# GpSimd takes two of the eight residual additions behind each of three outputs

## The reference

```python
h = modulate(rms_norm_2(x, g_pre_ff1), sh1, sc1)
f = swiglu(h, w1_gate, w1_up, w1_down)
x = x + 0.5 * ga1[:, None, :] * rms_norm_2(f, g_post_ff1)      # first output
h = modulate(rms_norm_2(x, g_pre_mix), sh2, sc2)
...                                                            # attention and a state space branch
x = x + ga2[:, None, :] * rms_norm_2(mixed, g_post_mix)        # second output
h = modulate(rms_norm_2(x, g_pre_ff2), sh3, sc3)
f = swiglu(h, w2_gate, w2_up, w2_down)
x = x + 0.5 * ga3[:, None, :] * rms_norm_2(f, g_post_ff2)      # third output, the result
```

## Time and profile before

| what | us |
|---|---|
| median of 3 runs | 3137.19 (3136.27 to 3139.3) |
| profiled execution, its own time | 3139.77 |
| span of the profiled execution | 3137.7 |
| PE busy | 3002.3 (96%) |
| DVE busy | 1722.9 (55%) |
| ACT busy | 1008.0 (32%) |
| POOL busy | 217.0 (7%) |

### The profile page before, as it was taken

One profiled execution on the slowest core, in us unless ns is written; L12 is line 12 of the kernel. 1 busy time (PEld: TensorE's weight loads), 2 busy tenths in 40 slices (PEclk: granted clock), 3 DMA queues, 4 the chain that ended last, 5 costly groups with the idle time before them and its releaser, 6 DMA issues.

```text
span 3137.7 us, 51509 instructions
## 1 busy us (share of the span) xinstructions
PE 3002.3 (96%) x21594; PEld 2569.2 (82%) x21594; DVE 1722.9 (55%) x3294; ACT 1008.0 (32%) x1737; POOL 217.0 (7%) x446
## 2 busy tenths in 40 slices
PE   8999999999999998999999999999999898899997
PEld 7777998999999997788998888878888655578886
DVE  4564577547656336447755765657447453543334
ACT  4556232232212236542323222233222314432122
POOL 0130222000000100212210000000000000000000
PEclk9999999999999999999999999999999999999999
DMA  5201111235433320111123453422334311123232
GB/s 186 99 15 48 52 60 60 75 136 168 161 118 124 122 94 28 52 44 61 60 77 137 156 184 118 161 74 94 114 104 147 145 45 37 54 78 105 86 102 73
DMA packets 74494, 302.45 MB, mean 96 GB/s; under 512 B 10729, under 2 KB 11113, under 8 KB 69273
## 3 DMA queue, kind: packets, MB, share of 16 engines
q1 hardware_dynamic: 57880, 230.04, 22.1%
q0 software_dynamic: 16384, 69.13, 6.1%
HBM read 288.51 MB, written 14.63 MB: 97 GB/s over the span
## 4 chain that ended last, share of the span: by engine, by line
PE 88%; DVE 6%; ACT 4%; issue 1%; DMA 1%; POOL 0%; DVEq 0%; SPq 0%; ACTq 0%
PE acc L1066 18%; PE acc L1067 18%; PE acc L1068 18%; PE acc L1385 5%; PE acc L1386 5%; PE acc L1387 5%; PE acc L1085 2%; PE acc L1267 2%; ACT temps L1812 1%; PE acc L1241 1%; PE acc L1214 1%; PE acc L1613 1%; PE acc L1430 1%; PE acc L1451 1%; PE acc L1121 1%
## 5 line engine op out<-in xcount | busy, mean ns | idle before, releaser
L1067 PE MATMUL acc<-normed_r,toep_r 128*128 128x512 f32 (+1 forms) x1808 | 636.5, 352 | 0.0
L1735 ACT ACTIVATE toep_r<-ring 128x1024 fp32r<-128x1024 f32 (+2 forms) x340 | 392.9, 1157 | 695.3 <-PE acc L1068 676.1
L2230 DVE TENSOR_TENSOR ring_r<-ring,toep_r 128x1024 fp32r<-128x1024 f32 (+2 forms) x340 | 457.9, 1348 | 261.3 <-ACT toep_r L1735 261.0
L1067 PEld LDWEIGHTS acc<-normed_r,toep_r 128*128 128x128 f32 x1808 | 341.4, 189 | 45.1 <-issue 0.2
L1066 PE MATMUL acc<-mixed_r,toep_r 128*128 128x264 f32 (+1 forms) x1056 | 343.2, 325 | 0.7 <-DVE normed_r L2213 0.6
L1066 PE MATMUL acc<-work_r,toep_r 128*128 128x512 f32 (+1 forms) x988 | 342.1, 346 | 1.5 <-DVE ring_r L2230 1.4
L1068 PE MATMUL acc<-work_r,ring_r 128*128 128x512 f32 (+1 forms) x988 | 341.4, 346 | 0.0
L1068 PE MATMUL acc<-mixed_r,ring_r 128*128 128x264 f32 (+1 forms) x1056 | 339.3, 321 | 0.0
L1066 PE MATMUL acc<-temps_r,toep_r 128*128 128x512 f32 x752 | 298.3, 397 | 11.0 <-DVE normed_r L2216 8.3
L1067 PE MATMUL acc<-work_r,toep_r 128*128 128x512 f32 (+1 forms) x880 | 307.7, 350 | 0.0
L1385 PE MATMUL acc<-residual_r,toep_r 128*128 128x264 f32 (+1 forms) x1024 | 301.9, 295 | 3.7 <-ACT toep L1952 2.1
(11 more groups left out here) (432 smaller groups left out, 5296.8 us busy)
## 6 DMA issues: line engine op xcount, KB each, us to landing
ring<-in_w_pair SPq DMA_DIRECT2D x176, 512.0 KB, 3.5
ring<-in_w_down SPq DMA_DIRECT2D x64, 704.0 KB, 4.1
ring<-in_w_gb SPq DMA_DIRECT2D x64, 640.0 KB, 3.9
extra<-in_w_ada POOLq DMA_DIRECT2D x18, 1024.0 KB, 5.9
toep<-in_w_ada POOLq DMA_DIRECT2D x18, 1024.0 KB, 5.8
ring<-in_w_tm SPq DMA_DIRECT2D x24, 512.0 KB, 4.5
ring<-in_w_out SPq DMA_DIRECT2D x24, 512.0 KB, 3.5
ring<-in_w_fm SPq DMA_DIRECT2D x20, 512.0 KB, 3.9
```

What stands on the lines that cost most here:

```text
L1067: mm(out, wh, xl[:, a:z], start=False, stop=False)
L1735: A(high(ld), slot(ld), ACT.Copy).then_inc(S["w_high"], 1)
L2230: V.tensor_tensor(low(ld), slot(ld), high(ld), ALU.subtract).then_inc(S["w_low"], 1)
```

## The change

Tiles 2 and 5 of each of the three outputs are added by POOL. DVE still scales them, reports each on a new semaphore `term_made`, and goes on with the next tile without a wait; POOL waits for it, adds, and reports on `pool_added`. The list of what the next norm or the store waits for names `pool_added` for these two tiles. SP waits for both tiles of a pair. To have room for the two semaphores, four older ones become two (`start_args`, `start_exp`), `ang_ready` is folded into `ssm_args`, and an unused one goes.

```diff
+POOL_ADDS = (2, 5)
...
+            n["done"] = [mark("pool_added" if adds and i in POOL_ADDS else signal) for i in tiles] if signal else None
+            n["terms"] = [mark("term_made") for _ in POOL_ADDS] if adds else None
...
-        b2["post1"] = norm(Y, b2["ffn1"]["ready"], range(KT), TOKENS, "h_done", total=TMP)
+        b2["post1"] = norm(Y, b2["ffn1"]["ready"], range(KT), TOKENS, "h_done", total=TMP, adds=True)
...
+            def additions(n):
+
+                for event, k in zip(n["terms"], POOL_ADDS):
+                    wait(pool, event)
+                    nc.gpsimd.tensor_tensor(H[:, k, META:L], H[:, k, META:L], n["src"][:, k, META:L], ALU.add
+                                            ).then_inc(S["pool_added"], 1)
...
                 second_block()
+                for name in ("post1", "postmix", "post2"):
+                    additions(b2[name])
...
                 for i, k in enumerate(n["tiles"]):
-                    link(V.scalar_tensor_tensor(out=n["src"][:, k, a:z], in0=n["src"][:, k, a:z],
-                                                scalar=g[:, i:i + 1], in1=RINV[:, a:z], op0=ALU.mult, op1=ALU.mult))
+                    term = V.scalar_tensor_tensor(out=n["src"][:, k, a:z], in0=n["src"][:, k, a:z],
+                                                  scalar=g[:, i:i + 1], in1=RINV[:, a:z], op0=ALU.mult, op1=ALU.mult)
+                    if i in POOL_ADDS:
+                        term.then_inc(S["term_made"], 1)
+                        continue
+                    link(term)
...
-                    act.wait_ge(S["ang_ready"], 1)
+                    act.wait_ge(S["ssm_args"], 2)
...
-                act.wait_ge(S["lb_shift"], 1)
+                act.wait_ge(S["start_args"], 1)
...
-                act.wait_ge(S["lam_dots"], 1)
+                act.wait_ge(S["start_args"], 2)
...
-                wait(sp, b2["post2"]["done"][2 * i + 1])
+                for k in range(2 * i, 2 * i + 2):
+                    wait(sp, b2["post2"]["done"][k])
```

More of the change, by code:

```diff
@@ L453, in build @@
         names += """means_loaded params_loaded start_loaded consts_loaded params2_loaded row_ready masked_row_ready line_stored row_spread toep_loaded
-            constants_set start_used lb_shift lb_exp lam_dots lam_exp cact_ready""".split()
+            constants_set start_used start_args start_exp cact_ready""".split()
         names += """sq_ready sq_used mean_read stat_ready stat_rooted gate_scaled silu_ready""".split()
-        names += """weights_made joint_mean u_ready h_done f_done fm_ready tm_ready gate_ready act_ready
+        names += """weights_made joint_mean u_ready h_done f_done fm_ready tm_ready act_ready
             hidden_ready""".split()
@@ L475, in build @@
             o_spread o_scaled dmix_ready""".split()
-        names += """u_shifted proj_full proj_read dt_ready ssm_args ssm_tanh ssm_sin ang_ready fc_ready ba_ready b_turned bt_staged ssm_made
+        names += """u_shifted proj_full proj_read dt_ready ssm_args ssm_tanh ssm_sin fc_ready ba_ready b_turned bt_staged ssm_made
             bt_loaded waves_loaded ca_loaded kd_cleared k_made kd_ready bu_ready bu_read scanned z_ready
             ssm_out ssm_y gelu_ready half_bias ssm_ready""".split()
+        names += """term_made pool_added""".split()
         names += """vector_chain scalar_chain pool_chain out_stored""".split()
@@ L548, in build, with norm @@
         norms = []
-        def norm(src, ready, tiles, pieces, signal="u_ready", total=None, bank=6, to=0, squared=True, inverse=None):
+        def norm(src, ready, tiles, pieces, signal="u_ready", total=None, bank=6, to=0, squared=True, inverse=None,
+                 adds=False):
             n = dict(total=total, n=len(norms), src=src, ready=ready, tiles=tiles, pieces=pieces, to=to,
@@ L555, in norm @@
                      inverse=RINV if inverse is None else inverse)
-            n["done"] = [mark(signal) for _ in tiles] if signal else None
+            n["done"] = [mark("pool_added" if adds and i in POOL_ADDS else signal) for i in tiles] if signal else None
+            n["terms"] = [mark("term_made") for _ in POOL_ADDS] if adds else None
             norms.append(n)
@@ L700, in build @@
             j.freed = mark("f_done")
-        b2["postmix"] = norm(Y, [j.freed for j in b2["out"]], range(KT), TOKENS, "h_done", total=TMP)
+        b2["postmix"] = norm(Y, [j.freed for j in b2["out"]], range(KT), TOKENS, "h_done", total=TMP, adds=True)
         b2["pre2"] = norm(H, b2["postmix"]["done"], range(KT), TOKENS)
         b2["ffn2"] = ffn(b2["pre2"], T8, ins["w2_pair"], ins["w2_down"], TOKENS, "f_done", bias=mod[:, 48:56])
-        b2["post2"] = norm(Y, b2["ffn2"]["ready"], range(KT), TOKENS, "h_done", total=TMP)
+        b2["post2"] = norm(Y, b2["ffn2"]["ready"], range(KT), TOKENS, "h_done", total=TMP, adds=True)
         att, groups = [], []
@@ L2030, in start_exp @@
             def start_exp():
-                act.wait_ge(S["lb_shift"], 1)
+                act.wait_ge(S["start_args"], 1)
                 lbv = st[:, START["lb"][0]:START["lb"][1]]
-                A(lbv, lbv, ACT.Exp).then_inc(S["lb_exp"], 1)
+                A(lbv, lbv, ACT.Exp).then_inc(S["start_exp"], 1)
             def start_lambda():
-                act.wait_ge(S["lam_dots"], 1)
-                A(lamt[:, 4:8], lamt[:, 0:4], ACT.Exp).then_inc(S["lam_exp"], 1)
+                act.wait_ge(S["start_args"], 2)
+                A(lamt[:, 4:8], lamt[:, 0:4], ACT.Exp).then_inc(S["start_exp"], 1)
                 A(cact, part(par, PARAMS, "c_cols"), ACT.Silu).then_inc(S["cact_ready"], 1)
@@ L2696, in start @@
                 link(V.tensor_tensor(la, la, lo, ALU.subtract))
-                V.tensor_tensor(lb, lb, lo, ALU.subtract).then_inc(S["lb_shift"], 1)
+                V.tensor_tensor(lb, lb, lo, ALU.subtract).then_inc(S["start_args"], 1)
                 low_weights(w[6])
-                dve.wait_ge(S["lb_exp"], 1)
+                dve.wait_ge(S["start_exp"], 1)
                 link(V.tensor_tensor(lo, la, lb, ALU.add))
@@ L2709, in start @@
                 link(V.tensor_tensor(prod, lv[:, :, 0, :], lv[:, :, 1, :], ALU.mult))
-                V.tensor_reduce(lamt[:, 0:4], prod, AX, ALU.add).then_inc(S["lam_dots"], 1)
+                V.tensor_reduce(lamt[:, 0:4], prod, AX, ALU.add).then_inc(S["start_args"], 1)
                 low_weights(w[7])
-                dve.wait_ge(S["lam_exp"], 1)
+                dve.wait_ge(S["start_exp"], 2)
                 for l in range(DEPTH):
@@ L2766, in ssm_step @@
                     angles(1, COARSE, "t3", "coarse")
-                    dve.sem_inc(S["ang_ready"], 1)
+                    dve.sem_inc(S["ssm_args"], 1)
                 elif i == 3:
```

## The result

| | before | after |
|---|---|---|
| median, us | 3137.68 (3136.19 to 3142.49, 19 runs) | 3142.59 (3140.33 to 3146.0, 19 runs) |
| span of the profiled execution | 3137.7 | 3142.6 |
| its own time | 3139.77 | 3144.68 |

The ratio of the medians, as the comparison of runs on one chip gives it, is 1.0014 with a 95% interval of 1.0008 to 1.0020: the change costs 4.4 us, between 2.5 and 6.3. That is within 0.2%, and the interval is clear of no change. I had forecast 3138.7 us, +1.5. On the earlier median of 3137.19 the ratio gives 3141.6; the new kernel's own median, 3142.59, stands 0.4 above my range. So the sign was right, the change stays within 0.2% as forecast, and my size was a third of the measured one. Where the rest is, the trace shows.

A forecast was written before the change was run, and what follows sets the result against it. DVE's scalings and additions were taken to bound the stretch behind each output. Six moved additions, each 0.97 us stood less 0.72 saved, give +1.5 us on 3137.19: 3138.7 us, 8 in 10 between 3135.2 and 3142.2.

The forecast's parts named there:

- What bounds the stretch: Behind the three outputs: DVE's eight scalings and eight additions stand on the path, one tile every 1.39 us.
- The two additions that leave DVE: DVE's row behind each output: each moved addition saves 0.72 us, six of them 4.3 us.
- What one costs on POOL: POOL's addition of 128x512: estimated at 1.27 us, bounds 1.00 and 1.46.
- What it costs DVE: Additions 3 and 6 stand 0.97 us each while POOL holds the way to SBUF; net +0.25 us per moved addition.
- no hold: Rival, all three outputs: POOL adds at 1.27 us, DVE goes on undisturbed; -3.4 us, 3133.8; chance 0.10.
- a starved GpSimd: Rival: POOL gets in only behind addition 7 of each output; +7.2 us, 3144.4; chance 0.04.
- The gain that the prediction sets beside the ratio of 1.27 to 0.69: POOL against DVE addition time: that ratio alone, without the hold, would still leave the gain of the second rival (the clock).
- Is the rest hidden?: Squares, means and stores behind DVE's row: square 7 still released by DVE, all behind shifts 0.5 us, stores don't meet.
- The clock stays low: Rival: TensorE's clock falls in PE's hole before mean 5 behind two outputs; 3143.1 us at most; chance 0.09.
- The sum: Whole kernel: 3 outputs x 2 additions x (0.97 - 0.72) = +1.5 us, median 3138.7 us.
- Something else: Rival, place left open, such as a shift of the code that moves many small waits; no size given; chance 0.05.
- The bounds and the spread that the prediction names: Forecast's range: POOL's time bounds give 3137.1 to 3139.8; three runs spread 0.9 below, 2.1 above their median.

The follow-up runs named there:

- the order with early tiles: Against the kernel before: all three outputs, RINV in PSUM, DVE scales five tiles in a row while GpSimd adds tiles 0 and 1; 3134.64 against 3138.57, 0.9989.
- the kernel with early tiles behind output 3 alone: Against the kernel before: only output 3 has five scalings in a row, tiles 0 and 1 on GpSimd, RINV in PSUM; 3136.58 against 3138.51, 0.9996.
- the pair of kernels that differ in the buffer of `RINV`: Against the kernel before: five scalings in a row, GpSimd adding tiles 0 and 1, with RINV in PSUM (0.9989) or in SBUF (1.0005).

## Why the prediction was right in sign and too small

- **What bounds the stretch.** Right. The rows of DVE set the last square in the changed kernel too, and what DVE gains or loses came through in full behind each output.
- **The two additions that leave DVE** (0.72 each). Right: the two scalings in a row take 1.41 us, and 18 additions are left.
- **What one costs on POOL** (1.27, bounds 1.00 and 1.46). Right: 1.266 us where nothing stands in the way (`RINV` in PSUM). The record beside DVE was forecast at 1.73, and is 1.70.
- **What it costs DVE** (stands 0.97). Nearly right: 1.636 - 0.692 = 0.94 us. The reading of the earlier trace rows, one pair of instructions of another kind, gave the size to 0.03 us. Net 0.22 instead of 0.25 us a tile; six are 1.32, not 1.5 us. The rivals of no hold and of a starved GpSimd are both gone with that. (The gain that the prediction sets beside the ratio of 1.27 to 0.69 is that of its first rival, no hold, and not of the second.)
- **Is the rest hidden?**, up to the last square. Right: squares 2 and 5 are released by POOL, 7 by DVE, all of it within 0.15 us of the times given, counted from the first scaling. First scaling to the end of the last addition: 11.63 us, forecast 11.7.
- **The clock stays low.** The hole of 1.3 us ahead of mean 5 was there (2495.9 to 2497.2), and the granted clock was 1.00 in it and in the rest of the norm. The rival fell in the first output, and in the second as well, where PE's hole around 2745 left the clock at 1.00. What is new is a longer fall behind the first norm: the clock was half from 2502.5 to 2509.3, where before it was so from 2501.6 to 2505.0. It didn't cost: the stretch that holds it, to the first scaling of output 2, was 0.37 us shorter than before.
- **Is the rest hidden?**, at the end. This is the step that failed. I looked at the stores, found rightly that they don't meet, and let everything behind the last addition stand at its 3.18 us. I took POOL's additions of tiles 2 and 5 as ended when their data were there. The missing term is what POOL still has to do when its last instruction is over: 8.02 us, which in the kernel before lay 638 us ahead of the end, at a place where nobody waits. The change moved POOL's last work from 2485.44 to 3134.37, and the term came to light: 3134.37 + 8.02 + 0.23 = 3142.62, against 3136.31 + 3.18 = 3139.49, +3.13 us.
- **The sum.** +1.5 forecast; +1.32 of it measured under the name that I gave it, +3.13 from the missing term, 4.45 in all. "Something else" had 0.05, and it was the larger part. That the change stayed within 0.2% as forecast is owed to the size of the missing term, 3 us in 3138, and not to my account of the end. (The bounds and the spread that the prediction names, put together, give 3136.2 to 3141.9 and not 3136.3 to 3141.)

A question could have found it: which engine now has its last instruction later than before, and what comes behind the last instruction of each? The 8.02 us could not have been read from the views of the kernel before, but the end-of-program wait could, and the move of POOL's last work by 650 us was plain in the diff.

What stays open: why GpSimd takes these 8.02 us, and why, in the order with early tiles, TensorE stood at half clock for twice as long behind output 1 as behind output 2. The runs show both, and explain neither. The order isn't all of it: in the kernel with early tiles behind output 3 alone, DVE made all additions behind output 2 as before, and the clock was half there from 2730.5 to 2737.3, twice as long as in the kernel before. It cost nothing, since DVE's row set the last square (11.29 us).

## What to carry to other kernels

Work given to an engine that had been done long ago also moves the end of its stream, so look at what each engine does behind its last instruction, and put late work on GpSimd only if its last instruction ends early enough: here it had to be 8.25 us ahead of the program's end. An elementwise pass moved from DVE to GpSimd gains only if DVE's neighbours with two inputs in SBUF stand for less time than the pass took: here 0.72 us were saved a tile, and 0.94 us stood with `RINV` in SBUF, 0.51 with it in PSUM. Before moving one, list the inputs of its neighbours, and put one in PSUM or choose another order, as the pair of kernels that differ in the buffer of `RINV` shows (-2.8 and +1.0 us by the rows, -3.5 and +1.6 by the runs). When the engine in the lead is made faster, the next one is close behind: here PE's means took over, and a third tile on GpSimd changed nothing more.

## What the runs showed of the hardware that I had not expected

- GpSimd's DRAIN at the end of the program lasts 8.01 to 8.02 us behind its last instruction, in twelve traces, whether that was an addition of 1.27 or 1.70 us, a copy or a MEMSET of 0.10 us. In the two traces where GpSimd's last work is the MEMSET of the earlier trace rows, with two transfers of its own still in flight, it was 14.2 and 14.4 us. The wait for it is shown under another engine's name.
- A GpSimd copy of 128x512 with a single input holds DVE's two-input addition as its own addition does: 0.29 us, for a copy of about 0.63 us (1.07 less the 0.44 that the addition waits, an estimate).
- ACT's root, two passes of 128x512, is faster in PSUM: the first reads PSUM and takes 0.66 us when it writes PSUM, 0.69 when it writes SBUF; the second takes 0.58 us within PSUM and 0.63 within SBUF.
